# Gathering tokens for two experts at once, clearing the accumulators ahead of the copies, and a row of maxima broadcast through DRAM

## The reference, cut to what matters

```python
b = cumsum(log_sigmoid(f_pre)); ig = i_pre
d = where(causal, b[t] - b[s] + ig[s], -inf)
m_t = maximum(b[t] + m, d.max(-1))
s = (q @ k.T) * exp(d - m_t[..., None])
num = s @ v ; den = s.sum(-1)
h = num / maximum(abs(den), exp(-m_t))
```

```python
logits = t @ w_router + b_router
top_v, top_i = lax.top_k(logits, 2)
top_w = softmax(top_v)
combine = sum(one_hot(top_i, 8) * top_w[..., None], axis=1)
for e in range(8):
    y += combine[:, e:e+1] * ((silu(t @ w1[e]) * (t @ w3[e])) @ w2[e])
```

## Time and profile before

| | |
|---|---|
| median of three runs | 2487.19 us (2484.70 to 2491.62) |
| the profiled execution: time / span of its trace | 2489.2 us / 2487.4 us |
| PE busy | 2407.0 us, 97% |
| DVE, ACT, POOL busy | 1685.7 us, 1233.3 us, 436.4 us |
| chain that ended last | PE 89%, DVE 5%, ACT 3%, issue 1%, POOL 1% |
| granted PE clock, mean | 0.974 |
| expert loop | about 1668 to 2480 us of the span |
| head steps of the mLSTM | about 938 to 1005 us (layer 0), 1579 to 1614 us (layer 1) |

### The profile page before, as it was taken

One profiled execution on the slowest core, in us unless ns is written; L12 is line 12 of the kernel. 1 busy time (PEld: TensorE's weight loads), 2 busy tenths in 40 slices (PEclk: granted clock), 3 DMA queues, 4 the chain that ended last, 5 costly groups with the idle time before them and its releaser, 6 DMA issues.

```text
span 2487.4 us, 35121 instructions
## 1 busy us (share of the span) xinstructions
PE 2407.0 (97%) x13490; PEld 2008.3 (81%) x13514; DVE 1685.7 (68%) x1931; ACT 1233.3 (50%) x1471; POOL 436.4 (18%) x359
## 2 busy tenths in 40 slices
PE   8999999999999998899999999889999999999998
PEld 6669998879998866678888887578888888888887
DVE  7555864466854766467655348658888888888887
ACT  5454334444333354332222144447777777777775
POOL 1003541004520000010003500003122131121221
PEclk9999999999999998899999989989999999999999
DMA  6564554414552310135555332028989989989895
GB/s 237 213 244 163 187 187 148 150 60 154 186 196 87 105 43 1 48 121 188 201 196 185 127 107 97 1 88 313 369 333 353 357 333 363 347 339 370 332 363 208
DMA packets 71605, 503.59 MB, mean 202 GB/s; under 512 B 8208, under 2 KB 8720, under 8 KB 11536
## 3 DMA queue, kind: packets, MB, share of 16 engines
q1 hardware_dynamic: 70272, 496.68, 54.6%
q0 software_dynamic: 1168, 4.66, 0.5%
HBM read 500.26 MB, written 1.05 MB: 202 GB/s over the span
## 4 chain that ended last, share of the span: by engine, by line
PE 89%; DVE 5%; ACT 3%; issue 1%; POOL 1%; DMA 0%; SPq 0%; DVEq 0%; ACTq 0%
PE ps L466 85%; PE ps L530 1%; DVE h L2189 1%; POOL h_r L1433 1%; PE ps L1252 1%; DVE ring_r L2216 1%; DVE h_r L2183 1%; PE ps L785 1%; DVE temp L2281 0%; PE ps L634 0%; ACT ring_hi L1551 0%; DMA cols<-in_cols 0%; DVE temp L2552 0%; ACT h L1599 0%; DVE h L2801 0%
## 5 line engine op out<-in xcount | busy, mean ns | idle before, releaser
L1551 ACT ACTIVATE ring_hi<-ring 128x2048 fp32r<-128x2048 f32 x427 | 807.1, 1892 | 566.6 <-PE ps L466 345.4
L2988 DVE TENSOR_TENSOR ring_r<-ring,ring_hi 128x2048 fp32r<-128x2048 f32 x264 | 617.6, 2346 | 121.0 <-ACT ring_hi L1551 119.1
L466 PE MATMUL ps<-ring_hi,extra_r 128*128 128x512 f32 (+2 forms) x1808 | 607.9, 392 | 6.9 <-DVE ring_r L2216 4.8
L2216 DVE TENSOR_TENSOR ring_r<-ring,ring_hi 128x2048 fp32r<-128x2048 f32 (+3 forms) x163 | 380.3, 2340 | 180.2 <-ACT ring_hi L1551 166.2
L466 PE MATMUL ps<-extra_r,ring_hi 128*128 128x256 f32 (+1 forms) x1432 | 461.1, 322 | 8.4 <-DVE ring_r L2216 4.6
L466 PE MATMUL ps<-extra_r,ring_r 128*128 128x256 f32 (+1 forms) x1432 | 457.5, 319 | 0.0
L466 PE MATMUL ps<-h_r,ring_hi 128*128 128x256 f32 (+2 forms) x1400 | 445.1, 318 | 0.0
L466 PE MATMUL ps<-ring_r,extra_r 128*128 128x512 f32 (+2 forms) x1104 | 422.7, 383 | 0.0
L466 PEld LDWEIGHTS ps<-ring_hi,extra_r 128*128 128x128 f32 x1808 | 341.3, 189 | 80.5 <-DVE ring_r L2216 6.0
L466 PEld LDWEIGHTS ps<-extra_r,ring_hi 128*128 128x128 f32 x1432 | 273.4, 191 | 32.4 <-DVE ring_r L2216 5.2
L466 PEld LDWEIGHTS ps<-extra_r,ring_r 128*128 128x128 f32 x1432 | 273.3, 191 | 19.0
(11 more groups left out here) (372 smaller groups left out, 3014.0 us busy)
## 6 DMA issues: line engine op xcount, KB each, us to landing
ring<-in_experts SPq DMA_DIRECT2D x264, 1024.0 KB, 4.9
ring<-in_stream SPq DMA_DIRECT2D x202, 1024.0 KB, 4.9
ring<-in_stream SPq DMA_DIRECT2D x6, 512.0 KB, 3.7
ring<-in_stream SPq DMA_DIRECT2D x2, 576.0 KB, 3.6
res<-in_xT SPq DMA_DIRECT2D x2, 512.0 KB, 4.1
res<-in_ctxT POOLq DMA_DIRECT2D x1, 1024.0 KB, 7.3
h<-in_consts POOLq DMA_DIRECT2D x2, 512.0 KB, 5.1
areaB<-in_cond_rows POOLq DMA_DIRECT2D x1, 1024.0 KB, 6.3
```

What stands on the lines that cost most here:

```text
L466: return pe.matmul(o, l, r, start=start, stop=stop, skip_group_check=True)
L1551: return act.activation(dst, src, ACT.Copy)
L2216: L.send(TTN(ring_lo[:, s, 0:n], ring[:, s, 0:n], ring_hi[:, j % HIS, 0:n].bitcast(F32), ALU.subtract), "weights_lo")
L2988: TTN(ring_lo[:, s, :], ring[:, s, :], ring_hi[:, j % HIS, :].bitcast(F32), ALU.subtract).then_inc(sig("weights_lo"), 1)
```

## The change

The change has three parts.

1. **Gather for two experts.** `pick` now holds two experts side by side (`[t, e % 2, slot]`), so one matmul of a gather has 256 columns instead of 128 and serves both experts. A call of `gather` fills a bank with two column blocks for two experts (four matmuls) instead of four blocks for one (eight matmuls). Experts 0 and 1 are gathered ahead of the loop with eight calls over four banks; experts 2 and 3 during expert 1, and so on: only the odd experts carry gathers, at j = 1, 2, 3, 4, 6, 7, 8, 9. `xexp` grows from two to three places per part (`room`), and its high part moves to another array. DVE makes the picks of two experts together. There are as many copies out of the banks as before per pair of experts.
2. **Accumulators first.** The banks of the router, of `htok`'s transposes and of the rank product are now fixed (4 and 5, 0 to 3, 6), so the accumulators 4 to 7 can be cleared before DVE has copied the tokens out; 10 `keep_warm` matmuls are put ahead of the clearing, and those ahead of the rank product go from 10 to 7.
3. **Maxima through DRAM.** PE's "lm" products and their banks go away. POOL writes `mrow` (16 KB) once per layer to a scratch tensor in DRAM, waits for it, and then issues one transfer per step, which reads one row of 256 floats into all 128 partitions (128 KB) of a double-buffered `lmax` in SBUF. The transfer of step n waits until ACT has finished the exponentials of step n-2. DVE and ACT read `lmax` instead of the bank.

```diff
+        lmax = area(areaB, 5632, 2, T)
+        mrow_out = nc.dram_tensor("mrow_out", (2, 4, 2, 2 * T), F32, kind="Internal").ap()
...
-        pick = area(areaA_r, 2816, 2, TT, P)
+        pick = area(areaA_r, 2816, TT, 2, P)
...
-        xexp = [area(extra, 2048 * i, 2, KD, P) for i in range(2)]
+        xexp = [area(areaA_r, 3328, 3, KD, P), area(extra, 0, 3, KD, P)]
+        room = [0, 1, 0, 2, 0, 1, 0, 2]
...
+        GATHER_AT = {1: 0, 2: 1, 3: 2, 4: 3, 6: 4, 7: 5, 8: 6, 9: 7}
...
-                    u = take("lm", l, n, bank=4 + n % 2)
-                    full(mm(ps[:, u.bank, 0:T], cst[0:4, CST["sel4"] + x * P:CST["sel4"] + (x + 1) * P],
-                            mrow[0:4, d, sq * T:(sq + 1) * T]), u)
...
-            us = [take("router", t) for t in range(TT)]
+            us = [take("router", t, bank=4 + t) for t in range(TT)]
...
-                    u = take("htok", t, g)
+                    u = take("htok", t, g, bank=2 * t + g)
...
-            u = take("rank")
-            keep_warm(u, 10)
+            u = take("rank", bank=6)
+            keep_warm(u, 7)
...
             moe_acc = [take("moe_acc", q, bank=4 + q) for q in range(4)]
+            keep_warm(moe_acc[0], 10)
             pe.wait_ge(sig("zero_ready"), 1)
...
-            def gather(bank, e, half, w_):
-                for k in range(4):
+            def gather(bank, x):
+                f, w_ = divmod(x, 2)
+                for k in range(2):
                     for t in range(TT):
-                        kk = 4 * half + k
-                        m = mm(ps[:, bank, k * P:(k + 1) * P], htok[w_][:, t, kk * P:(kk + 1) * P], pick[:, e % 2, t, :],
-                               t == 0, t == TT - 1)
+                        kk = 2 * f + k
+                        m = mm(ps[:, bank, k * T:(k + 1) * T], htok[w_][:, t, kk * P:(kk + 1) * P],
+                               pick[:, t, :, :].rearrange("p e s -> p (e s)"), t == 0, t == TT - 1)
...
-                pe.wait_ge(sig("pick"), i * (2 * NE) + 2)
-                gather(0, 0, 0, 0)
-                gather(1, 0, 0, 1)
-                gather(2, 0, 1, 0)
-                gather(3, 0, 1, 1)
+                pe.wait_ge(sig("pick"), i * (2 * NE) + 4)
+                for x in range(8):
+                    if x >= 4:
+                        pe.wait_ge(sig(("xexp_hi", "xexp")[x % 2]), i * (2 * NE) + (x // 2 - 1))
+                    gather(x % 4, x)
                 pe.wait_ge(sig("combine"), 1)
-                pe.wait_ge(sig("xexp_hi"), i * (2 * NE) + 1)
-                gather_share(0, 0)
-                pe.wait_ge(sig("wcur"), i * (2 * NE) + 2)
+                pe.wait_ge(sig("xexp_hi"), i * (2 * NE) + 4)
+                gather_share(2, 0)
...
+                pool.wait_ge(sig("lrows"), l + 1)
+                pool.dma_start(mrow_out[l], mrow[0:4, :, :]).then_inc(sig("mrow_out"), 16)
+                pool.wait_ge(sig("mrow_out"), 16 * (l + 1))
+                for n, (sq, x, d) in enumerate(lsteps(l)):
+                    if n >= 2:
+                        pool.wait_ge(sig("lexp"), 16 * l + n - 1)
+                    pool.dma_start(lmax[:, n % 2, :], mrow_out[l, x, d, sq * T:(sq + 1) * T].partition_broadcast(P)
+                                   ).then_inc(sig(f"lmax{n % 2}"), 16)
...
-                    u = look(dve, "lm", l, n)
+                    L.wait(f"lmax{n % 2}", 128 * l + 16 * (n // 2 + 1))
...
-                    if c == 6:
+                    if e % 2 and c == (6 if e == NE - 1 else 0):
                         picks((e + 1) % NE)
+                        picks((e + 2) % NE)
```

More of the change, by code:

```diff
@@ L1996, in exponentials @@
                     own = lw[n % 2][:, ns - 2:ns, :]
-                    u = uses["lm", l, n]
-                    if ns > 2:
-                        for i in range(ns - 2):
-                            L.go(act.activation(lw[n % 2][:, i, :], ps[:, u.bank, 0:T], ACT.Exp,
-                                                bias=lc[:, STILES[sq][i], 0, d, x:x + 1], scale=-1.0))
-                    leave(act.activation(own, own, ACT.Exp, scale=-1.0), u)
+                    for i in range(ns - 2):
+                        L.go(act.activation(lw[n % 2][:, i, :], lmax[:, n % 2, :], ACT.Exp,
+                                            bias=lc[:, STILES[sq][i], 0, d, x:x + 1], scale=-1.0))
+                    L.send(act.activation(own, own, ACT.Exp, scale=-1.0), "lexp")
                 def sum_att(t):
@@ L2115, in _ @@
                 expert_hi(i, 0)
-                for half in range(2):
-                    act.wait_ge(sig("gather_full"), i * (5 * NE) + (2 * half + 1))
-                    gathered(0, half, 2 * half)
+                for f in range(4):
+                    act.wait_ge(sig("gather_full"), i * (5 * NE) + (2 * f + 1))
+                    gathered(0, f, 2 * (f % 2))
                 expert_hi(i, 1)
@@ L2784, in exponents @@
                         a = ns - 2 + i
-                        ins = STT(out=lw[n % 2][:, a, :], in0=ps[:, u.bank, 0:T], scalar=lc[:, STILES[sq][a], 0, d, x:x + 1],
+                        ins = STT(out=lw[n % 2][:, a, :], in0=lmax[:, n % 2, :], scalar=lc[:, STILES[sq][a], 0, d, x:x + 1],
                                   in1=lmask[:, d, i, :], op0=ALU.subtract, op1=ALU.max)
@@ L2793, in weights @@
                     sq, x, d = steps[n]
-                    left(dve, "lm", l, n)
+                    L.wait("lexp", 16 * l + n + 1)
                     if n >= 2:
@@ L2959, in _ @@
             picks(0)
+            picks(1)
             for g in range(2):
```

82 lines of the change are left out of this document (47 added, 35 removed).

## The result

The kernel after took 2458.24 us, median of four runs (2453.86 to 2468.87), against 2487.10 for the kernel before: ratio 0.9887, interval 0.9872 to 0.9901. It is 28.9 us faster where I had forecast 17.6, and lies 1.8 us under the low end of my range. The direction and the largest term were right; one term was far off. The profiled execution took 2459.3 us (span 2457.5), 29.9 less than that of before.

The account below looks back on a forecast made before the run. PE was taken as the bound (97% busy), DVE and transfers close behind. Loop -13.2, entry -3.7 and head steps -0.7 gave -17.6 us, hence 2470.6 us, between 2471.6 (profiled execution) and 2469.6 (median); range 2460 to 2484.

Parts of the forecast that it names:

- my range: Whole kernel: the measured time was to lie from 2460 to 2484 us.
- Loop, -13.2: Expert loop: 24.4 us of 128-column gathers removed, 11.2 us of 256-column gathers added; bounds -13.9 and -3.4.
- Entry, -3.7: Entry of the expert loop: earlier clearing and gathers; middle of -2.6 (clock falls) and -4.8 (clock holds); bounds -1.4 and -6.
- Start of the steps, -3.2 per layer: Start of each layer's head steps: copies go, 2.6 us, and scores move before the clock's fall, 0.6.
- The copies' own 2.6 us: Start of each layer: two copies of 1.1 us and a third of 1.5 us go from PE.
- the scores move before the fall of the clock, 0.6: Start of each layer: the scores run ahead of the clock's fall, worth 0.6 us per layer.
- The 2.4 us that I had kept as a side bound: Start of each layer: up to 2.4 us more saved if the clock no longer falls at all.
- Length of the transfer, 4.2 us: Head steps: each transfer of maxima takes 4.2 us from issue to landing; each us more costs 8 us in all.
- +5.7: Head steps after the start: +1.2 us per layer in four-tile steps, +3.3 in layer 0's two-tile steps.
- My lower bound, 3.1 us: Head steps: with transfers of 3.1 us the steps fall back on PE and DVE, about -6 against the forecast value.
- the row of the same size: Head steps: the profile's one 128 KB transfer from POOL, from which the transfer's length was put at 4.2 us.
- Both unspent bounds: Head steps: savings left out of the sum, up to 2.4 us for the clock, about 6 for transfers of 3.1 us.

Follow-up runs that it names:

- e10: The kernel after without the 10 keep-warm products ahead of the clearing of the accumulators; 2461.6 us.
- e5: The kernel after with POOL clearing 128x1024 floats ahead of each transfer of maxima, from the third step of each layer on; 2468.6 us.
- e6: The kernel after with four places for rows of maxima instead of two, the transfer of step n waiting for the exponentials of n-4; 2454.7 us.
- e8: The kernel after with PE's 24 copies of the maxima back in their places, read by nobody; 2475.3 us.
- e14: The kernel after with idle copies of the maxima, read by nobody, in the first three places of each layer only; 2475.7 us.
- e13: The kernel after with three keep-warm products in each of the places of the first three copies of each layer, read by nobody; 2462.8 us.
- e4: The kernel before with the 12 keep-warm products of each layer's head steps moved ahead of the first scores; 2491.2 us.
- e2: The kernel before with the second part alone (fixed banks, accumulators cleared ahead); 2482.6 us.
- e3: The kernel before with the first part alone (gathers for two experts at once); 2471.7 us.
- e9: The kernel before with the first and second parts (paired gathers and fixed banks), PE still copying the maxima; 2473.1 us.

## Why the prediction was wrong

- **Loop, -13.2: right.** -13.5 in the trace; prices, unchanged cover and even the 363 GB/s came out as worked out.
- **Entry, -3.7: right in number for the stretch, in part by luck.** -4.4. The clock held, which I had left open, but in this execution it fell just ahead of the stretch, which the sum did not look at, and 3.6 us went back there. Over both the gain was 0.8 us, and about 3 by the other kernels. A fall inside the entry costs what I had put, 2.2 us, more or less: 1.1 in e10, 2.1 to 3.0 in e5, e6 and e8.
- **Start of the steps, -3.2 per layer: the step that failed.** Measured -7.2 and -7.5. The copies' own 2.6 us is right. I wrote "the scores move before the fall of the clock, 0.6", and so kept the fall itself, ahead of the 12 keep-warm products, as if nothing in the change could take it away. It was the work of the copies that I was taking away (e8, e14 against e13). In layer 1 the scores fall from 5.4 to 2.9 us: 1.6 us of that is the clock and 0.9 the row of scores that is no longer broken (e13), and against these 2.5 us I had 0.6. The keep-warm products fall by another 2.1. The 2.4 us that I had kept as a side bound covered only these. That is 8.3 us of the miss. Against the mean of the twelve starts with copies, 11.8 us, the gain is 6.3 per layer, and 6.1 us of the miss; the rest is that the kernel before was profiled with two long starts.
- **Length of the transfer, 4.2 us: the wrong value of a right term.** It is 3.2 us (3.1 to 3.5 over 24), and e5 gives 8.5 us per us where I had 8. At 3.2 the steps changed by +0.4 us in both layers together, where the sum had +5.7: 5.3 us of the miss, as far as one execution of each tells. My lower bound, 3.1 us, was the better guide; I took the row of the same size. That one reads 128 rows of DRAM and this one a single row of 1 KB, 128 times; whether this makes the difference no run shows. By this trace, with its 3.2 us, the Trainium skill's fit in "DMA: Bandwidth & Descriptors", section "Anatomy of one DMA — SWDGE (gpsimd) path", an estimate of 2.3 us for 128 KB, is too short here too, though its consequence (the sum at my lower bound) is the one that came.
- **The rest.** The entry was 0.7 and the loop 0.3 us better than forecast, and all else +2.3 us worse: 8.3 + 5.3 + 0.7 + 0.3 - 2.3 is the 12.3 us between 29.9 and 17.6. Outside the way to the rank product, "all else" is -1.2 us in untouched places and not explained further.
- **The range** was too narrow on one side. Both unspent bounds, the clock and the short transfer, lay on the fast side, and the low end took in the keep-warm products' 2.4 us once. Twice, for both layers, it would have been near 2459, and with the scores as measured 2455.

Left open: what in a four-row float32 product brings the clock down (its rows, its type or its two passes were not tried apart); what brings it down ahead of the rank product (e4, without either of the first two parts, shows it too, and e2 does not); and why e3 alone gave 17 us, 5 more than its loop (12.1 in its trace), if its interval does not cover that.

## What to carry to other kernels

A fall of PE's clock in the trace before is an effect, and the change may remove its cause: look at what PE ran just ahead of it, and ask whether the edit takes that away. When a bank's product becomes a transfer, look for the ring that closes through its buffers; two more places cost nothing here and took the transfer's length out of the sum. Parts that each shorten the same stretch are not added: two of them gave 4.7 and 3.6 us alone and 4.4 together. And a stretch in which the clock now holds is read together with the one ahead of it, where the fall may have gone.

## What the runs showed of the hardware

- Three products of 4 rows by 256 columns in full float32, 1.7 us in all, went with 3 to 10 us at the 1.2 GHz level in all twelve starts of the six kernels that had them there (before, e2, e3, e8, e9, e14); bf16 products of 128 rows in their place did not (e13, granted clock 1.00 for 20 us from the first scores on, in both layers), and in the 18 starts of the nine other kernels without copies the clock was never down before the first value product, 4.8 to 5.5 us on. Where it fell, it was back by the first value product or early in it.
- Eight scores of 64 rows by 256 columns took 2.90 us in one row (after) and 1.92 + 1.93 us in two halves with other products between, both at clock 1.00 (e13).
- The clock fell at other places in every execution (985 to 1005 us of the span: 0.50 to 0.71 in every kernel). A saving can move such a fall: e4 saved 7.6 us at the two starts and lost 9.9 in the steps, and the kernel after holds 1.00 in the entry and has 0.66 in the ten us ahead of it.
- POOL's transfer of one row to 128 partitions (128 KB) took 3.2 us from issue to landing, 3.1 to 3.5 over 24 of them, the one out of SBUF (16 KB) 4.5 us, and issuing one held POOL 0.54 us.
